# Expert blocks of 64 tokens in f32 on two 64-column tiles, with the experts sorted by count on the chip

## What is computed

```python
pg = softmax(hf @ w_rg + b_rg);  g_sel = argmax(pg);  p_gsel = pg[g_sel]
le = (hf @ w_re + b_re).reshape(n, 4, 8);  le_sel = le[:, g_sel]
top_p, top_i = top_k(softmax(le_sel), 2)
gate_w = p_gsel * top_p / sum(top_p);  experts = g_sel * 8 + top_i
...
y[token] += gate_w * ((silu(x @ w_gate[e]) * (x @ w_up[e])) @ w_down[e])
```

## Time and profile before

| | us |
|---|---|
| runs | 3978.57, 3983.18, 3979.01 (median 3979.01) |
| span of the profiled execution | 3984.4 |
| PE busy | 3570.6 (90%) |
| DVE busy | 2429.7 (61%) |
| ACT busy | 1549.1 (39%) |
| POOL busy | 229.4 (6%) |

### The profile page before, as it was taken

The page is one execution under the profiler, slowest core; times in us unless marked ns, Lnnn a source line. Parts: engine busy times, 40 slices in busy tenths (PEclk is TensorE's granted clock), DMA queues, the critical chain, the costliest instruction groups (busy, mean ns, idle before and its releaser), DMA issues. The chain is left out here.

```text
span 3984.4 us, 53126 instructions
## 1 busy us (share of the span) xinstructions
PE 3570.6 (90%) x18991; PEld 2777.6 (70%) x18991; DVE 2429.7 (61%) x3047; ACT 1549.1 (39%) x1977; POOL 229.4 (6%) x421
## 2 busy tenths in 40 slices
PE   7999995899999598785999996998899989779997
PEld 4535674788888487564888885876687768558876
DVE  2126654788888623655888886544655575355554
ACT  2004642677777302634777774012210021121101
POOL 0000110111111100001111111000000000000000
PEclk9999997999999799997999997998899988989999
DMA  7075913999997324007999994220332255013321
GB/s 265 35 278 138 248 42 115 350 366 388 373 366 287 127 75 96 1 22 260 351 361 366 365 365 154 97 69 22 95 97 93 63 86 82 24 48 100 98 92 53
DMA packets 390766, 688.59 MB, mean 173 GB/s; under 512 B 63508, under 2 KB 261985, under 8 KB 384359
## 3 DMA queue, kind: packets, MB, share of 16 engines
q1 hardware_dynamic: 368972, 655.55, 49.7%
q0 software_dynamic: 21024, 30.86, 2.2%
q10 hardware_dynamic: 627, 0.24, 0.0%
HBM read 661.74 MB, written 70.52 MB: 184 GB/s over the span
## 5 line engine op out<-in xcount | busy, mean ns | idle before, releaser
L2131 DVE TENSOR_TENSOR moe0b_w_lo<-moe_raw,moe0b_w_hi 128x2048 fp32r<-128x2048 f32 x118 | 264.5, 2289 | 60.4 <-ACT moe0b_w_hi L2035 57.7
L2131 DVE TENSOR_TENSOR moe1b_w_lo<-moe_raw,moe1b_w_hi 128x2048 fp32r<-128x2048 f32 x112 | 251.1, 2288 | 58.1 <-ACT moe1b_w_hi L2035 55.7
L2035 ACT ACTIVATE moe0b_w_hi<-moe_raw 128x2048 fp32r<-128x2048 f32 x118 | 218.9, 1922 | 26.2 <-PEq L1514 26.2
L2035 ACT ACTIVATE moe1b_w_hi<-moe_raw 128x2048 fp32r<-128x2048 f32 x112 | 207.9, 1922 | 21.5 <-PEq L1514 21.5
L556 ACT ACTIVATE ln_squares<-all_x 128x512 f32<-128x512 f32 x32 | 19.3, 632 | 371.7 <-DVE all_x L606 371.7
L1938 PE MATMUL moe0b_gate_ps<-moe0b_w_hi,moe0b_feats_hi 128*128 128x512 f32 x264 | 110.4, 418 | 9.8 <-DVE moe0b_feats_lo L2137 5.7
L1938 PE MATMUL moe1b_gate_ps<-moe1b_w_hi,moe1b_feats_hi 128*128 128x512 f32 x256 | 107.0, 418 | 9.8 <-DVE moe1b_feats_lo L2137 5.7
L2131 DVE TENSOR_TENSOR moe0b_w_lo<-all_h,moe0b_w_hi 128x2048 fp32r<-128x2048 f32 x48 | 107.2, 2287 | 1.5 <-PE moe0b_up_ps L1938 1.5
L2131 DVE TENSOR_TENSOR moe1b_w_lo<-all_h,moe1b_w_hi 128x2048 fp32r<-128x2048 f32 x48 | 107.2, 2286 | 1.3 <-PE moe1b_up_ps L1938 1.3
L1938 PE MATMUL moe0b_gate_ps<-moe0b_w_lo,moe0b_feats_hi 128*128 128x512 f32 x264 | 104.1, 394 | 0.0
L1938 PE MATMUL moe0b_up_ps<-moe0b_w_hi,moe0b_feats_hi 128*128 128x512 f32 x264 | 104.0, 394 | 0.0
(11 more groups left out here) (669 smaller groups left out, 10222.5 us busy)
## 6 DMA issues: line engine op xcount, KB each, us to landing
moe_raw<-in_moe_w_gate SPq DMA_DIRECT2D x166, 512.0 KB
moe_raw<-in_moe_w_up SPq DMA_DIRECT2D x166, 512.0 KB
all_h<-in_moe_w_down SPq DMA_DIRECT2D x128, 512.0 KB
moe_raw<-in_moe_w_down SPq DMA_DIRECT2D x128, 512.0 KB
all_ahead<-in_ffn_w_up SPq DMA_DIRECT2D x88, 512.0 KB, 5.1
all_ahead<-in_moe_w_gate SPq DMA_DIRECT2D x62, 512.0 KB
all_ahead<-in_moe_w_up SPq DMA_DIRECT2D x62, 512.0 KB
y_rows<-all_zero SPq DMA_DIRECT2D x43, 512.0 KB, 6.7
```

The lines of the kernel that those rows point to most:

```text
L2035: A_.activation(w_hi[r % HIGH][:], raw[slot][:], ACT.Copy).then_inc(rounded, 1)
L2131: V.tensor_tensor(w_lo[r % SPLIT][:], raw[r % RAW][:], w_hi[r % HIGH][:].bitcast(F32), ALU.subtract).then_inc(split, 1)
```

## The change

- **Blocks.** SLOTS is 64. A new `ExpertPlan` lists the visits (one visit is one block of one expert): experts 0 and 1 are at ranks 0 and 1; the other ranks go by falling count, found on the chip. In layer 0 the first ten ranks have two visits and rank 2 has three, the other 22 have one: 43 visits. In layer 1 the first eight have two and the other 24 one: 40 visits. Rows that find no room in these run in a loop under a condition, of up to 23 or 15 blocks, and with these inputs none does. An expert with several visits has its weights loaded once.
- **Sorting.** DVE computes a key from each expert's count, how many keys are larger, and the expert of each rank (`order`). SP reads `order` before each expert's loads.
- **Products.** All are plain f32, straight from the loaded pieces: nothing is rounded or split any more on ACT and DVE. With 64 rows in a block, one 64-column tile of the array takes gate and the other up (`wide_half`); in `down_half` the two tiles take the two halves of the output's columns. A visit has 24 matmuls of 64x512, in 12 pairs, and 12 transposes of 64 rows.
- **Weights.** One DMA of 1 MB per piece, with runs of 8 KB per partition. The ring has 18 slots (13 of its own, 3 in `P.h`, 2 in `P.ahead`). The router's inputs and the 12 pieces of experts 0 and 1 are started by the normalisation stage (`RouteInputs.start`), the next five in `route` once `order` is there.
- **Rows.** The gathers take 64 rows of 4 KB, from two buffers; the results are stored by an indirect DMA of 128 half rows of 2 KB. `clear_rows` has 33 DMAs where it had 43.
- The blocks are written out one after the other, with no loop over experts.

```diff
-SLOTS = 128
+SLOTS = 64
...
+    RING = 18
+    OWN = 13
+
+    def __init__(self, n_tok):
+        self.doubles, self.third = (10, 1) if n_tok == TOK else (8, 0)
...
+    def start(self, sp):
+        sp.dma_start(self.w_route[:, :, 0:N_GROUPS], rows_of(self.A["moe_w_rg"][self.l])).then_inc(self.w_in, 16)
...
+        for n in range(FIXED * PIECES):
+            self.weights.fetch(sp, n, self.plan.order[n][0])
...
+                    link(V.scalar_tensor_tensor(key[:], counts, float(E), inputs.tie[:], ALU.mult, ALU.add))
+                    link(V.tensor_tensor(larger, key[:].unsqueeze(1).to_broadcast([PART, E, E]),
+                                         key[:].unsqueeze(2).to_broadcast([PART, E, E]), ALU.is_gt))
+                    link(V.tensor_reduce(place_of[:], larger, AX.X, ALU.add))
+                    link(V.scalar_tensor_tensor(match[:], place_of[0:E, :], inputs.number[0:E, :], count[0:E, 0:E], ALU.is_equal, ALU.mult))
+                    link(V.tensor_reduce(order_f[:], match[:], AX.X, ALU.add))
+                    V.tensor_copy(order[:], order_f[:]).then_inc(order_ready, 1)
...
+                def wide_half(n, gate, up, h):
+                    for c in range(4 * h, 4 * h + 4):
+                        at = slice((c % 4) * D_EXPERT, (c % 4 + 1) * D_EXPERT)
+                        nc.tensor.matmul(wide_ps[n][LOW, :], feats[n][:, c, :], gate[:, at], start=c == 0, stop=c == DC - 1)
+                        last = nc.tensor.matmul(wide_ps[n][HIGH, :], feats[n][:, c, :], up[:, at], start=c == 0, stop=c == DC - 1)
+                    return last
+
+                def down_half(n, rows, j):
+                    for c in range(2 * j, 2 * j + 2):
+                        at = (c % 2) * D
+                        nc.tensor.matmul(result_ps[n][LOW, :], columns[n][:, c, :], rows[:, at:at + BANK], start=c == 0, stop=c == EC - 1)
+                        last = nc.tensor.matmul(result_ps[n][HIGH, :], columns[n][:, c, :], rows[:, at + BANK:at + D], start=c == 0, stop=c == EC - 1)
+                    return last
...
+                    for n in range(plan.RING - 1, len(plan.order)):
+                        if plan.order[n][0] != loaded:
+                            loaded = plan.order[n][0]
+                            e = chosen_expert(loaded)
+                        if n >= plan.RING:
+                            sp.wait_ge(used, plan.freed[plan.order[n - plan.RING]])
+                        weights.fetch(sp, n, e)
...
+                    for s in range(N):
+                        if s:
+                            hidden_rows(s - 1)
+                        wide(s)
+                        if s + 1 < N:
+                            rows(s + 1)
+                        if s:
+                            down(s - 1)
```

More of the change, by code:

```diff
@@ L1438, in out_stage, with __init__ @@
     split_stage(nc, P, tag, o, slabs, products, first, engines=("dve",))
-def extra_blocks(n_tok):
-    return (2 * n_tok - 2) // SLOTS
-BLOCKS_MAX = N_EXPERTS + extra_blocks(TOK)
-UNUSED = float(1 << 20)
-def expert_stage(nc, A, K, P, l, first_tok):
+FIXED = 2
+PIECES, WIDE_PIECES = 6, 4
+PIECE = 4 * D_EXPERT
+class Visit:
+    def __init__(self, rank, turn, number):
+        self.rank, self.turn, self.number = rank, turn, number
+class ExpertPlan:
+    RING = 18
+    OWN = 13
+    def __init__(self, n_tok):
+        self.doubles, self.third = (10, 1) if n_tok == TOK else (8, 0)
+        self.extra = (2 * n_tok - 2) // SLOTS
+        self.main = N_EXPERTS + self.doubles + self.third
+        self.blocks = self.main + self.extra
+        self.most = -(-n_tok // SLOTS)
+        heavy, light = list(range(FIXED, self.doubles)), list(range(self.doubles, N_EXPERTS))
+        ranks = list(range(FIXED)) + heavy + light
+        self.visits = []
+        for rank in ranks:
+            self.visits.append(Visit(rank, 0, rank))
+            if rank < self.doubles:
+                self.visits.append(Visit(rank, 1, N_EXPERTS + rank))
+            if self.third and rank == FIXED:
+                self.visits.append(Visit(rank, 2, N_EXPERTS + self.doubles))
+        self.count = len(self.visits)
+        phases = []
+        for s in range(self.count + 1):
+            if s < self.count:
+                phases += [("wide", s, h) for h in range(2)]
+            if s:
+                phases += [("down", s - 1, j) for j in range(2)]
+        self.order, self.freed, self.done = [], {}, {}
+        for n, (what, s, part) in enumerate(phases):
+            rank = self.visits[s].rank
+            for k in ((2 * part, 2 * part + 1) if what == "wide" else (WIDE_PIECES + part,)):
+                if (rank, k) not in self.freed:
+                    self.order.append((rank, k))
+                self.freed[rank, k] = n + 1
+            self.done[what, s, part] = n + 1
+        self.at = {piece: n for n, piece in enumerate(self.order)}
@@ new lines, in expert_stage, with gather @@
+        rows_in = [sb(f"rows_in{n}", [SLOTS, D]) for n in range(2)]
+        token_now = sb("token_now", [SLOTS, 1], I32)
+        gathered, stored = P.pool_sems[l][0:2], P.pool_sems[l][2:4]
+        y_halves = P.y_dram[0:BLOCKS * SLOTS, :].rearrange("r (h n) -> (r h) n", h=2)
+        def gather(rows, tokens, into):
+            nc.gpsimd.indirect_dma_start(rows, None, P.h_dram[0:n_tok, :], bass.IndirectOffsetOnAxis(ap=tokens, axis=0),
+                                         bounds_check=n_tok - 1, oob_is_err=False).then_inc(into, 16)
@@ L1513, in route, with gather_visit, chosen_expert @@
+        def gather_visit(s):
+            at = plan.visits[s].number
+            gather(rows_in[s % 2][:], slot_token[0:SLOTS, at:at + 1], gathered[s % 2])
+        def chosen_expert(rank):
+            return rank if rank < FIXED else nc.sync.value_load(order[rank:rank + 1, 0:1], min_val=0, max_val=N_EXPERTS - 1)
+        norm_stage(nc, P, f"ffn{l}", modulate_jobs(P, l, 1, spans), 0, ahead=inputs, squares_in=P.ahead)
         def route():
@@ L1745, in _ @@
+                    link(V.tensor_tensor(block_of[:], block_of[:], over[:], ALU.mult))
+                    link(V.tensor_tensor(block_of[:], block_of[:], own[:], ALU.add))
                     dve.sem_inc(placed, 1)
@@ L1788, in blocks_run @@
[L1788 to L1790 removed]
+                LOW, HIGH = slice(0, SLOTS), slice(SLOTS, PART)
+                feats = [sb(f"feats{n}", [PART, DC, SLOTS]) for n in range(2)]
+                hidden = [sb(f"hidden{n}", [PART, D_EXPERT]) for n in range(2)]
+                columns = [sb(f"columns{n}", [PART, EC, SLOTS]) for n in range(2)]
+                result = [sb(f"result{n}", [PART, BANK]) for n in range(2)]
```

848 lines of the change are left out of this document (355 added, 493 removed).

## The result

| | before | after |
|---|---|---|
| median of the runs, us | 3980.62 (3978.57 to 3983.18) | 3952.50 (3951.64 to 3954.26) |
| span of the profiled execution | 3984.4 | 3952.4 |
| PE busy | 3570.6 (90%) | 3439.3 (87%) |
| DVE busy | 2429.7 | 1465.5 |
| ACT busy | 1549.1 | 812.1 |

The change is faster, by a ratio of 0.9927 (95% interval 0.9913 to 0.9941), that is 28 us in the medians and 32 in the profiled spans. I had forecast 70. The time lies in the range I gave, but the gain is two fifths of the one predicted. Of four executions of the experiment e8 one took 8426 us, against 3904 to 3909 for the others, and is left out of its median.

The account below looks back on a forecast made before the run. PE was taken to pace the kernel before. Layer 0 −26.2, layer 1 −45.7 and +2 at the ends gave −70 us, from 3979 to 3909 us; likeliest 3885 to 3945 (0.62), outer range 3860 to 4000.

Parts of the forecast that it names:

- What bounds the kernel before: Expert stages before the change: PE paces at 17.90 us an expert, the DMA engines a little below what they can do.
- PE per visit: Expert blocks: 12 pairs at 0.86 us, transposes 1.57, changes of tile shape 0.5; together 12.4 us of PE a visit.
- The second rival: Expert blocks: late rows or hidden rows, or a fallen clock, lengthen visits by 1 to 3 us; 3946 to 4020 us, chance 0.10.
- Third and fourth rival: Expert products: weight loads not hidden, about 4362 us (chance 0.03); tiles don't run beside each other, about 4669 us (0.02).
- The stream per light expert: Light phase: weights at 418 GB/s take 15.05 us, rows 0.9 or 0.65; 16.0 us an expert in layer 0, 15.7 in layer 1.
- The first rival: Light phase: the stream runs at 369 GB/s, a light expert takes 18.0 us; 84 us worse, 3993 us, chance 0.09.
- + 2 for the last visit: End of each layer's light phase: 2 us added after the light experts' stream time for the last visit.
- the stores of the rows wait for nothing long: Layer 0 before the blocks: stores behind 12 pieces on SP, 30 us from about 640, wanted only near 686.
- the −3.6 that I had: Layer 0 route: PE's wait for a weight load goes, as normalisation now starts that load; 3.6 us less.
- Route of layer 1: Layer 1 before the blocks: PE's start of the expert stage moves from 1846.2 to 1849.7, 3.5 us later.
- there are more empty turns of the loop: +1 us each: End of each layer's blocks: indirect store replacing a direct one and more empty turns, +1 us each, +2 in all.
- One us more per light expert costs 42: Sensitivity of the total: one us more per light expert costs 42 us, one more per heavy-phase visit 37.

Follow-up runs that it names:

- e8: The change with only 2 of 64 rows gathered and 2 of 128 half rows stored in visits of one-visit experts (needed work left out): 3904.8 us.
- e2: The change with ACT's last exponential of route put ahead of its copies of rows 4 and 5: 3940.7 us, 11.8 less than the change.
- e1: The change with the loop for extra blocks under a condition of its own, so no empty turns: 3941.2 us, 11.3 less than the change.
- e7: The change with 8 instead of 10 ranks of two visits in layer 0, 4 instead of 8 in layer 1: 3904.0 us, 48.5 less than the change.
- e9: The change with each piece still one DMA of 1 MB, but in two runs of 4 KB a partition: 3972.6 us, 20.1 more than the change.
- e4: The change with each piece loaded by two DMAs of 512 KB with runs of 4 KB: 3972.2 us, 19.7 more than the change.
- e5: The change with each piece in two DMAs of 512 KB, cut by partitions, runs still 8 KB: 4205.0 us, 252 more than the change.

## Why the prediction went wrong, point by point

- **What bounds the kernel before; PE per visit.** Right. 12.4 us forecast, 12.25 measured in nearly every visit of the heavy part: pairs at 0.86 us, transposes and changes of shape together 1.9 where I had 2.1. The second rival (longer visits, or a fallen clock) did not come: the granted clock was 1.00 in the heavy windows and 0.94 and 0.96 in the light ones. Over the 21 and 16 heavy visits this gave 3.2 and 2.4 us more gain than forecast.
- **Third and fourth rival.** Neither came, as the trace of the router's product had it. Two weight loads of 0.14 us lie in each step of 0.43 us and delay nothing: two steps are the 0.86 us that the columns alone were reckoned at. The rule of the Trainium skill, "TensorE: Matmul & The Clock Gate", part 3, that a load overlaps matmuls in flight only with another row group, does not hold here.
- **The stream per light expert: right mechanism, term mis-sized.** 16.0 and 15.7 forecast. Without rows it is 15.24 (e8), where I took 15.05, and rows cost 1.08 and 0.86 where I took 0.9 and 0.65: 16.3 and 16.1 (the visits in the light parts show 16.2 and 15.9). Over 20 and 22 experts that is 6 and 9 us too little. The rows were sized from the share of POOL's queue at PE's pace. That share came out about right, 5.3% of 300 us or 0.9 us an expert; what it leaves out is that the pieces go at 404 GB/s beside the rows and at 415 without (e8). The first rival (369 GB/s) did not come: 409 to 411 in the light parts, 420 in e8. The 358 GB/s which the Trainium skill, "DMA: Bandwidth & Descriptors", section "Where 436 GB/s comes from", gives as what the HBM side binds at did not bind here, with one core alone running: the measured rates lie above it.
- **Layers 0 and 1, "+ 2 for the last visit": mis-sized.** PE's last wait for a piece in layer 0, the second half of the last expert's up, ends at 1287.14. Two down pieces of that expert are then still to come, 2.1 MB or 5.1 us at 409 GB/s, while PE works on: the rest of these products, the down half of the visit before, the turning of the hidden rows and the last down products, in this order. The last result is copied at 1299.02, 11.9 us after that wait, so by this estimate about 7 us behind the stream, 5 more than I had. In layer 1 it is about the same. The windows show the stream running out from 1288 on (the last three columns are granted clock, DMA share and GB/s):

```profile
1287.14 0.61 PE L1934 MATMUL moe0b_wide_ps<-moe_raw,moe0b_feats 128*64 128x512 f32 x1 [1.63 <-DMA moe_raw<-in_moe_w_up]
...
1288.00:1290.00 2.00, 2.00 (x12) 0.86 (x10) 0.00 (x0) 0.00 (x0) 0.00 (x0) 1.00 0.78 324
1290.00:1292.00 2.00, 2.00 (x12) 0.71 (x10) 0.55 (x1) 0.59 (x1) 0.00 (x0) 1.00 0.52 217
1292.00:1294.00 2.00, 2.00 (x12) 0.64 (x8) 0.14 (x1) 0.00 (x0) 0.00 (x0) 1.00 0.25 102
```

  With PE's faster visits and the slower pieces from above, −3.2 + 6 + 5 = 8 for layer 0 and −2.4 + 9 + 5 = 12 for layer 1, against the 9.4 and 11.2 of the table.
- **Layer 0, "the stores of the rows wait for nothing long": the step that failed outright.** I asked when the last store is wanted (by the gather) and not who waits for an earlier one. The rows have four buffers for six rows, so ACT waits for the first store, which lands behind 12.6 MB of weights, and the exponential behind ACT's copy holds DVE for 11.2 us, where it had been 1.7. e2 gives back 9.6; then norm and route are as long as before the change (65.3 against 65.1), 4 less than I had forecast. PE's first product of the router stands 18.4 us behind the first square there, against 22.3, the −3.6 that I had; from it to PE's first work of the blocks it is 46.9 us against 42.8, so that the 7.5 for what DVE and POOL do more was 4.1.
- **Route of layer 1.** +5.5 where I had 3.5, a figure for which I had shown no sum. The trace tells where: the router's first product stands 14.7 us behind the first square against 16.4, only 1.8 gained where layer 0 gained 3.9, and from there to the first work of the blocks it is 42.0 us against 34.7, 7.3 more. Which of the steps behind it costs that no run tells; it stays open.
- **The end, "there are more empty turns of the loop: +1 us each": failed.** 0.43 us a turn, 23 and 15 turns, and no cover: the store before them is POOL's own now, where SP's did it before. e1 shows 7.8 and 4.2 us. I had given them and the indirect store 1 us a layer together, with no working, as if they were hidden as before.
- **Sensitivities.** "One us more per light expert costs 42" and the two-phase sum were right in kind: e7 came out at 48.5 for 50 by the same sum. e8 took about 1.0 and 0.7 us off a light visit and gained 48 us, more than the 20 x 1.0 + 22 x 0.7 = 35 of that rule.
- **The size of what I called likely.** What I called likeliest was 3885 to 3945, with a chance of 0.62, and the time is 3952.5. Most of the errors had the same sign (PE's pace and the work in route went the other way), and I had widened upward only for a slow stream or slow visits. That the time still lies in the outer range is no merit of the mechanism: the range was wide enough for the first rival, which did not come.

## What to carry to other kernels

When a change splits a stage into a part that one resource paces and a part that another does, first ask whether they can be mixed: here that alone was worth 82 us where the change itself gave 28. Work out for each resource what it needs over the whole stage first, as the larger sum is about the floor: in layer 1 it was the stream's 509 us and not PE's 490. A transfer put earlier on a queue delays everything that is issued behind it, so ask for the first one that somebody waits for, and what stands behind that waiter in its own program. And a loop that does nothing costs its turns, 0.43 us each here, as soon as it has lost the wait that hid it.

## What the runs showed of the hardware that I had not expected

- DMAs of 1 MB over 128 partitions with runs of 8 KB move 409 to 411 GB/s in the light part, with the rows beside them; with runs of 4 KB it is 400 to 402, whether the piece is one DMA or two (e9, e4). Over both stages that is 20 us.
- DMAs of 512 KB over 64 partitions, with the same runs of 8 KB, move 344 GB/s in layer 0's light part and 246 in layer 1 between 2100 and 2300 us, while the engines count as full (e5).
- Scattered rows cost more than their bytes: 10.9 MB of them are 27 us at 409 GB/s and cost 44 us of blocks (e8). Without them the total rate is 420 GB/s and an expert takes 0.86 to 1.08 us less.
- Two f32 tiles of 64 columns with 512 columns streamed run beside each other at 0.86 us a pair, with their weight loads hidden, for whole visits on end.
